# Folding a sum of squares to 64 partitions, and a norm one slot later, in a macaron encoder kernel on eight cores

## The reference, cut to what matters

```python
h = x + 0.5 * swiglu(rmsnorm(x, norm_ffn1), w_gate1, w_up1, w_down1)      # FFN 1, hidden width 2816
u = rmsnorm(h, norm_mix); p = u @ w_in                                    # 512 pooling + 5 x 512 recurrence columns
h = h + concat(pool_mixer(p), bidirectional_recurrence(p)) @ w_out
h = h + 0.5 * swiglu(rmsnorm(h, norm_ffn2), w_gate2, w_up2, w_down2)      # FFN 2
out = rmsnorm(h, norm_final)

def rmsnorm(x, w):      # over the 1024 channels of each token
    return x * rsqrt(mean(x * x, axis=-1) + 1e-6) * w
```

## Time and profile before

| what | us |
|---|---|
| median of 3 runs | 4908.35 (4901.43 to 4914.44) |
| the profiled execution | 4901.7 |
| span of its slowest core (core 6), first to last instruction | 4900.2 |
| spans of the 8 cores | 4886.7 to 4900.2 |
| TensorE matmul busy | 4738.6 (97%) |
| VectorE busy | 2382.0 (49%) |
| ScalarE busy | 1507.8 (31%) |
| GpSimd busy | 608.2 (12%) |
| DMA, mean | 139 GB/s |

### The profile page before, as it was taken

One profiled execution on the slowest core, in us unless ns is written; L12 is line 12 of the kernel. 1 busy time (PEld: TensorE's weight loads), 2 busy tenths in 40 slices (PEclk: granted clock), 3 DMA queues, 4 the chain that ended last, 5 costly groups with the idle time before them and its releaser, 6 DMA issues.

```text
span 4900.2 us, 69795 instructions; the slowest of 8 cores (4886.7 to 4900.2 us)
## 1 busy us (share of the span) xinstructions
PE 4738.6 (97%) x23237; PEld 2221.8 (45%) x23704; DVE 2382.0 (49%) x3831; ACT 1507.8 (31%) x2386; POOL 608.2 (12%) x661
## 2 busy tenths in 40 slices
PE   7999999999999999999996899999999999999998
PEld 3444444444444444444443344444444444444443
DVE  3333333332344444666666566566666665244444
ACT  2222223222121113544553334343334343111111
POOL 1000000000000001333334212111211221000000
PEclk9999999999999999999998999999999999999999
DMA  8151111111479664444446554344444433534553
GB/s 170 72 121 54 74 57 71 74 56 64 156 239 252 218 211 157 141 160 161 151 160 151 146 152 125 121 142 144 121 134 130 147 117 117 159 146 185 194 194 127
DMA packets 211025, 682.32 MB, mean 139 GB/s; under 512 B 21488, under 2 KB 67952, under 8 KB 181360
## 3 DMA queue, kind: packets, MB, share of 16 engines
q1 hardware_dynamic: 199152, 636.76, 38.5%
q0 software_dynamic: 11520, 41.06, 5.5%
HBM read 419.95 MB, written 298.84 MB: 147 GB/s over the span
## 4 chain that ended last, share of the span: by engine, by line
PE 90%; DMA 3%; DVE 3%; issue 2%; ACT 1%; POOL 1%; DVEq 0%; SPq 0%; another core or an unknown queue 0%; ACTq 0%; POOLq 0%
PE bank L254 89%; DMA HT<-arena 1%; DVE arena L239 1%; PE bank L257 1%; DMA arena<-x 1%; DVE arena L242 1%; ACT arena L236 1%; DMA PL<-arena 0%; POOL arena L239 0%; DVE arena L248 0%; DMA FB<-arena 0%; DVE arena L575 0%; ACT L236 0%; POOL sst L239 0%; DMA OF<-arena 0%
## 5 line engine op out<-in xcount | busy, mean ns | idle before, releaser
L254 PE MATMUL bank<-arena 128*128 128x512 bf16 (+1 forms) x22343 | 4683.1, 368 | 75.3 <-DVE arena L239 26.2
L254 PEld LDWEIGHTS bank<-arena 128*128 128x128 bf16 x22808 | 2153.1, 98 | 2512.5 <-issue 95.5
L239 DVE TENSOR_TENSOR arena<-bank,arena 128x512 bf16<-128x512 f32 (+1 forms) x896 | 617.9, 690 | 1230.6 <-PE bank L254 1039.2
L236 ACT ACTIVATE arena<-bank 128x512 bf16<-128x512 f32 (+1 forms) x1064 | 625.1, 594 | 1710.9 <-PE bank L254 1562.9
L236 ACT ACTIVATE arena<-arena 128x512 f32<-128x512 f32 (+1 forms) x1085 | 660.7, 625 | 1462.4 <-DVE arena L242 919.1
L239 DVE TENSOR_TENSOR arena<-arena 128x512 f32<-128x512 f32 (+2 forms) x592 | 399.7, 675 | 251.0 <-ACT arena L236 234.1
L242 DVE SCALAR_TENSOR_TENSOR arena<-bank,arena 128x512 f32<-128x512 f32 x256 | 176.8, 691 | 618.3 <-PE bank L254 563.6
L239 POOL TENSOR_TENSOR arena<-arena 128x527 f32<-128x527 f32 (+7 forms) x294 | 351.9, 1201 | 654.9 <-ACT arena L236 206.3
L242 DVE SCALAR_TENSOR_TENSOR arena<-arena,nwt 128x512 bf16<-128x512 f32 (+1 forms) x512 | 362.3, 745 | 12.6 <-ACT arena L236 12.6
L236 ACT ACT_TABLE_LOAD x164 | 210.4, 1283 | 91.8 <-PE bank L254 77.5
L242 DVE SCALAR_TENSOR_TENSOR arena<-arena 128x8 bf16<-128x8 f32 (+2 forms) x252 | 152.1, 624 | 104.5 <-ACT arena L236 78.0
(11 more groups left out here) (26 smaller groups left out, 361.3 us busy)
## 6 DMA issues: line engine op xcount, KB each, us to landing
HT<-arena SPq DMA_DIRECT2D x352, 256.0 KB, 2.1
arena<-HT SPq DMA_DIRECT2D x64, 1408.0 KB, 12.9
H<-arena SPq DMA_DIRECT2D x32, 2048.0 KB, 7.8
arena<-H SPq DMA_DIRECT2D x31, 2048.0 KB, 9.3
arena<-x SPq DMA_DIRECT2D x30, 2048.0 KB, 10.6
out<-arena SPq DMA_DIRECT2D x15, 2048.0 KB, 7.3
arena<-U SPq DMA_DIRECT2D x17, 1024.0 KB, 5.5
U<-arena SPq DMA_DIRECT2D x16, 1024.0 KB, 4.4
```

Of the source, the lines that this page charges most:

```text
L236: P.add("act", lambda e: e.activation(out=out, in_=in_, func=func, **kw), r=r, w=w)
L239: P.add(eng, lambda e: e.tensor_tensor(out=out, in0=in0, in1=in1, op=op), r=r, w=w)
L254: P.add("pe", lambda e: e.matmul(out, lhsT=lhsT, rhs=rhs, start=start, stop=stop), r=r, w=w)
```

## The change

Where the norm has tiles of its own (`tiles is None`: phases A, B and D), `hilo` first copies partitions 64 to 127 of ACC to partitions 0 to 63 of RS, adds them to the lower half of ACC, casts the sum to bf16 into the lower half of HI, and writes sum minus HI into the upper half of HI. `pe` is then one matmul with ones over HI. Phase C keeps two matmuls. In phase A, `pe`, `rs` and the eight `out` become steps 11, 12 and 13 to 20, and the two `when` tables are renumbered. In `Down.run`, `pe` and `rs` move from behind d = 0 into the matmuls of d = 1, in front of f = 8; the pass i = NB keeps them at d = 0. In phase C, for all blocks but the first two (i > 1), `pe`, `rs` and `out` come one slot later.

```diff
     class Norm:
         def __init__(self, cv, nwi, bank, tiles=None):
+            self.fold = tiles is None
...
         def hilo(self):
+            if self.fold:
+                A, R, W = self.ACC, self.RS, self.HI
+                cp(R.ap[0:64], A.ap[64:128], A.pg(), R.pg())
+                tt(A.ap[0:64], A.ap[0:64], R.ap[0:64], ALU.add, A.pg() + R.pg(), A.pg())
+                cp(W.ap[0:64], A.ap[0:64], A.pg(), W.pg())
+                tt(W.ap[64:128], A.ap[0:64], W.ap[0:64], ALU.subtract, A.pg() + W.pg(), W.pg())
+                return
             cp(self.HI.ap, self.ACC.ap, self.ACC.pg(), self.HI.pg())
             tt(self.LO.ap, self.ACC.ap, self.HI.ap, ALU.subtract, self.ACC.pg() + self.HI.pg(), self.LO.pg())

         def pe(self):
             b = banks[self.bank]
-            mm(b[:, :], ones[:], self.HI.ap, True, False, self.HI.pg() + [("ones",)], BK(self.bank))
+            mm(b[:, :], ones[:], self.HI.ap, True, self.fold, self.HI.pg() + [("ones",)], BK(self.bank))
+            if self.fold:
+                return
             mm(b[:, :], ones[:], self.LO.ap, False, True, self.LO.pg() + [("ones",)], BK(self.bank))
@@ phase_a, norm_steps
             st[9] = [nm.hilo]
-            st[10] = [nm.pe]
-            st[11] = [nm.rs]
+            st[11] = [nm.pe]
+            st[12] = [nm.rs]
             for k in range(NK):
-                st[12 + k] = [lambda k=k: nm.out(x, u, k)]
+                st[13 + k] = [lambda k=k: nm.out(x, u, k)]
@@ phase_a, start
-            when = {0: range(1, 5), 1: range(5, 10), 2: (10, 11), 3: range(12, 20)}
+            when = {0: range(1, 5), 1: range(5, 10), 2: (11, 12), 3: range(13, 21)}
...
-            when = {12: (1, 2), 13: (3, 4), 14: (5, 6), 15: (7, 8), 16: (9, 10), 17: (11, 12), 18: (13, 14), 19: (15, 16), 20: (17, 18), 21: (19,)}
+            when = {12: (1, 2), 13: (3, 4), 14: (5, 6), 15: (7, 8), 16: (9, 10), 17: (11, 12), 18: (13, 14), 19: (15, 16), 20: (17, 18), 21: (19, 20)}
@@ Down.run
                         for f in range(NF):
+                            if i > 0 and d == 1 and f == 8:
+                                nm.pe()
+                                nm.rs()
                             mm(banks[bk][:, :], WD[li].v(d * DP + f * 128, 128), ht.v(f * BT, BT), f == 0, f == NF - 1,
...
                         if d == 0:
-                            nm.pe()
-                            nm.rs()
+                            if b is None:
+                                nm.pe()
+                                nm.rs()
@@ make_c, mix
             put(o + 28, nm.hilo)
-            put(o + 29, nm.pe)
+            e = 30 if i > 1 else 29
+            put(o + e, nm.pe)
             put(o + 29, lambda: sp(H2_d[b], H.ap, H.pg(), [("dram", "H2", b)], ("c", "h2s")))
-            put(o + 30, nm.rs)
+            put(o + e + 1, nm.rs)
             for k in range(8):
-                put(o + 31 + k // 2, lambda k=k: nm.out(H, u, k))
+                put(o + e + 2 + k // 2, lambda k=k: nm.out(H, u, k))
```

## The result

The changed kernel takes **1.0028 times** the time of the one before, interval 1.0017 to 1.0038: about 14 us more, where the prediction had 7.6 us less. The executions that are compared lie between 4913.95 and 4925.28 us for the changed kernel and between 4899.26 and 4914.44 us for the one before; executions in which the cores of a die ran at a lower granted clock are left out, and where an experiment's profile has such cores, the others are read. The profiled execution took 4913.95 us, with a span of 4912.4 us on core 1 and 4902.7 to 4912.4 us over the cores. The 4900.7 us of the prediction were wrong, and the time is above its range.

A forecast was written before the change was run, and what follows sets the result against it. TensorE was taken as the bound, busy 97% of the span. The terms -9.5 + 2.7 + 2.7 - 2.4 - 1.7 + 0.7 - 0.4 + 0.3 = -7.6 us took 4908.35 to 4900.7 us, range 4888 to 4911.

The forecast's parts named there:

- Part 4: Phase C, later slot: waits for LO go, but a new 0.40 us wait at `kt` cancels them; -0.4 and +0.3 us.
- the upper bound of 5 us: Phase C: +5 us if the new wait at `kt` is twice the 0.40 us worked out.
- Part 1: Phases A, B and D: 48 matmuls go, 44 of them save 0.216 us each, -9.5 us.
- Part 2: Split 1.33 us longer, exposed only at ends of B and D (+2.7 us) and norms 0 and 1 (+2.7 us).
- Parts 2 and 3, the start: Folds of norms 0 and 1 +2.7 us; norm 2 loses its wait, -2.4, and half clock, -1.7; block 2 +0.7 us.
- 0 as the other end: Start: the +2.7 us of norms 0 and 1 vanish if the HT store's landing has a fixed time.
- The ends cost more: Rival: longer or remaining half clock at end of B and norm 2, copy at 0.80 us; +4.5, 4905.2 us; chance 0.13.
- Slower: one more pair of table loads: Rival, phase C: two more table loads per block in ScalarE's chain to `kt`, 33 us, 4934 us; chance 0.03.
- The late slot pays in C: Rival: late slot gains in phase C and the start's delay is absorbed, -5.3 and -2.7 us, 4892.7 us; chance 0.20.

## Why the prediction was wrong

**Part 4, the step that failed.** It reads "the multiply of slot 37 and then `qk` of head 3 ... in the rows that ends at 3300.38, now at 3301.27". The step took VectorE's durations from the rows of before, 0.68 us each, into an order where other work stands beside them. Nothing in it asked what GpSimd does between 3296.70 and 3299.7, though that line is in the same timeline. The ScalarE chain was right to 0.02 us, the place of the new wait was right, and its size without GpSimd is the predicted 0.40 us. With it the cost is 1.56 us a block. The term was +0.3 - 0.4 us and measures +15.0; the upper bound of 5 us was "twice that" and so rested on the same durations. An operation's duration had been taken as a constant of its shape, and that left out the one mechanism that decided.

**Part 1** held: 48 matmuls fewer, and 0.216 us for each of those in the steady parts of A and D. Phase B shows 2.3 us less of its 3.2; it also varies by 1 to 3 us between the kernels that share its code, so nothing is made of that.

**Part 2, the split.** Timeline of the changed kernel, end of phase B, then end of phase D, against the earlier trace rows:

```profile
1886.72 0.42 DVE L248 COPY arena<-arena 64x512 f32<-64x512 f32 x1
1887.60 0.68 DVE L239 TENSOR_TENSOR arena<-arena 64x512 f32<-64x512 f32 x1 [0.46 <-DVE arena L248]
1888.39 0.42 DVE L248 CAST arena<-arena 64x512 bf16<-64x512 f32 x1
1888.91 0.69 DVE L239 TENSOR_TENSOR arena<-arena 64x512 bf16<-64x512 f32 x1
...
1889.86 0.59 PE L254 MATMUL bank<-arena,ones 128*128 128x512 bf16 x1 [5.60 <-DVE arena L239]
...
4896.64 0.58 PE L254 MATMUL bank<-arena,ones 128*128 128x512 bf16 x1 [5.25 <-DVE arena L239]
```

The f32 copy takes 0.42 us, the duration of the cast, and copy and add are 0.52 + 0.79 = 1.31 us in norm 1 of this core (the predicted 1.33); here the add came 0.35 us later still. Half the partitions make nothing shorter. The Trainium skill (VectorE: DVE Perf Modes, "The perf-mode tier table (the rule you actually need)") gives an f32 copy within SBUF about twice the rate of an f32 operation with two inputs. The rows agree in direction: 0.42 against 0.68 us, 1.6 times. From the last matmul to the first `out` the end of B grew by 1.6 us and that of D by 1.1 us (medians 8.68 to 10.25 and 6.99 to 8.10), near the 1.33 each that was predicted; a product that waits by itself starts 0.26 us after VectorE's end (1889.60 to 1889.86). The place inside d = 1 showed no wait for the split in B or D.

**Parts 2 and 3, the start**, is the second term that was mis-sized. The prediction has +2.7 for two folds and -3.4 for norm 2, together -0.7 us; the three stretches give +7.3. Three things were off. Each fold costs 2.0 to 2.5 us on its own stretch and not 1.33 (1.7 to 2.2 where one was folded alone). At norm 2 the half clock was read from core 6 and credited to the kernel, and five of eight cores didn't have it. And the delay was let pass with "0 as the other end", at its own length at most, where it passes and then grows.

At norm 1, timeline and stretch (us, busy PE, PEld, DVE, ACT, POOL, PEclk) of the changed kernel, cores 7 and 1:

```profile
45.98 0.58 PE L254 MATMUL bank<-arena,ones 128*128 128x512 bf16 x1 [3.49 <-DVE arena L239]
```

```profile
45.00:51.50 6.50, 3.02 (x8) 1.20 (x9) 3.50 (x6) 2.28 (x4) 0.00 (x0) 0.70 1.02 185
```

TensorE stands for 3.5 to 3.9 us in all cores, where before it stood for 0.9 to 1.6 us in front of HI and 0.3 for LO, and behind it runs at the lower level, 1.2 GHz, in seven of the eight (not in core 6): on core 1 eight matmuls in 3.62 us from 48.86. No core had that at norm 1 before. The rival "The ends cost more" has this effect, but at the end of B and at norm 2, and with +4.5 us in all.

The third stretch grows by the wait for the HT store and the half clock behind it, as the table above shows. Timeline of core 1 after, then of core 1 before:

```profile
100.06 1.29 DVE L239 TENSOR_TENSOR arena<-bank,arena 128x512 bf16<-128x512 f32 x2 [14.78 <-DMA HT<-arena]
100.89 5.48 PE L254 MATMUL bank<-arena 128*128 128x512 bf16 x14 [4.47 <-DVE arena L239]
```

```profile
90.68 1.29 DVE L239 TENSOR_TENSOR arena<-bank,arena 128x512 bf16<-128x512 f32 x2 [11.49 <-DMA HT<-arena]
91.51 8.79 PE L254 MATMUL bank<-arena 128*128 128x512 bf16 x40 [1.18 <-DVE arena L239]
```

Behind 4.47 us of waiting a matmul takes 0.39 us, behind 1.18 us it takes 0.216. Why the store keeps TensorE waiting longer, when TensorE itself comes to it later, **stays open**.

**The rivals.** "Slower: one more pair of table loads" had the right sign and place and the wrong mechanism: ACT's count is 2386 in both kernels. "The late slot pays in C" needed no wait at `kt`, and there are two a block. A rival in which VectorE's moved work meets GpSimd's was missing. The row of 3.02 us for two equal multiplies, of which one alone takes 1.26, was its sign in the old trace.

## What to carry to other kernels

When a step moves in time, list what runs beside it in its new place on every engine, and look in the old trace for an operation that is longer than its equals: what stands beside it is what the moved step may meet. A wait of a few tenths of a microsecond is best removed by a few matmuls, not by a slot. And an operation saved on the bound engine is worth its 0.216 us only where that engine is fed; where it stands waiting, the longer way to the one product is paid in full, so fold in the steady part and not at the ends.

## What the runs showed of the hardware that was not expected

- A VectorE multiply with two inputs in SBUF that comes while GpSimd multiplies from SBUF ends 0.55 us after GpSimd's instruction: 1.75 us instead of 0.68 to 0.74. In the other order it is GpSimd's that is long, 1.79 or 1.71 us instead of 1.26.
- A product with ones that waits alone starts 0.26 us after VectorE's end (1889.60 to 1889.86); the transposes of `kt` start 0.14 us after it (3408.46 to 3408.60, 3409.66 to 3409.80). Why they differ was not tried.
- Behind the 3.5 us of waiting at norm 1 the granted clock fell in seven of eight cores; behind the 1.4 and 0.4 to 0.6 us at norm 2 of the kernel before it fell in three of eight; behind the 0.98 us at `kt` it did not: eight matmuls of 512 columns follow there in 1.89 us, 0.216 us from one to the next, and the granted clock from 3380 to 3440 us is 1.00.
